# A PSUM bank for every other matmul: two output chunks of a weight tile computed in turn

## Chip, cores and metric

The kernel runs on one core of a Trainium2 chip. The metric is the device time of one execution in microseconds (us); lower is better. TensorE is the matmul engine (PE in the profile, its weight loads are PEld), DVE is VectorE, ACT is ScalarE, POOL is GpSimd, and SP issues the weight transfers.

## The reference

What is computed is a chain of layers on 512 tokens of width 1024, all in fp32, each added to x:

```python
x = x + gated_deltanet_mixer(rms_norm(x, a_norm), ...)      # A: 8 heads, w_in then w_out
k_band, v_band = shared_kv(x, kv_norm, w_kv, k_gain)        # KV
x = x + swa_sink_mixer(rms_norm(x, b_norm), ...)            # B: 32 heads, w_in then w_out
x = x + 0.5 * swiglu_ffn(rmsnorm(x, g), w_in, w_out)        # FF 0
x = x + pool_mixer(rmsnorm(x, g), ...)                      # pool
x = x + 0.5 * swiglu_ffn(...)                               # FF 1
x = x + 0.5 * swiglu_ffn(...)                               # FF 2
x = x + conformer_conv(rmsnorm(x, g), ...)                  # conv: pw1 (I), depthwise, pw2 (O)
x = x + 0.5 * swiglu_ffn(...)                               # FF 3
return rmsnorm(x, final_g)

def swiglu_ffn(x, w_in, w_out):
    gate, up = jnp.split(x @ w_in, 2, axis=-1)
    return (jax.nn.silu(gate) * up) @ w_out
```

## The kernel before

Activations lie transposed in SBUF, channels on partitions and the 512 tokens along the free dimension: x is xT, eight chunks of 128 channels. Weights stream through as tiles of 128 x 2048 (1 MB) in two buffers. Every tile goes through the same steps: SP loads it (`load`, L325 to L328), ACT rounds it to fp32r in w_hi (`round_tile`, L335), DVE forms the rest w_lo (`split_tile`, L340), and TensorE multiplies. A product of two fp32 numbers is made of three fp32r matmuls: hi by hi, hi by lo and lo by hi (L359, L360, L361 in `products`).

There are two kinds of tile, and TILES lists their order. An input tile (I) holds 256 output channels of x @ w_in over the whole depth of 1024: two output chunks, each of eight terms, so 2 x 24 matmuls. Its chunks go to PSUM banks 0 and 1, those of the next input tile to 2 and 3. An output tile (O) holds 256 rows of w_out and all 1024 output channels: eight chunks, each of two terms, so 8 x 6 matmuls, into banks 4 to 7 in turn. A feed-forward layer (FF) is I I, then ten times I I O, then O; the two I of a step are the gate and the up tile.

`pe_tile` (L364) issues both kinds, one chunk after the other. Each finished chunk raises chunk_done. Its readers wait for chunk_done: for an output chunk DVE adds it to xT (`add_chunks`, L402, or L400 with a bias) and raises out_free; for FF input chunks ACT takes silu of the gate (L1583) and DVE multiplies (L1625), which raises in_free. TensorE waits for out_free before a chunk n of an output tile, so that the chunk four before it, in the same bank, has been added, and for in_free before an input tile, with all_free for all banks. Two other places compute input tiles: `arriving` (L346 to L351) for the first tile of a layer, which takes each term as its h arrives and does three matmuls for one bank and three for the other; and `pe_filler` (L680 to L682), which places single terms between other work in A and B. Neither is touched.

After the last output tile of a layer the next norm begins: ACT squares each chunk of xT (L433), DVE sums the squares (`dve_sum`, L465, one after every add from the third chunk on, and L472 for the last), TensorE sums over partitions (`pe_stat`, L440), ACT takes the root (L457), DVE inverts and widens (L478, L480), TensorE spreads (L447), and DVE and ACT make h (L499, L510, L503).

All engines run their own program in order. In A's output tiles DVE has convolution taps (L1017, L1020) between adds 4 to 7 of the first tile and a weight split before the adds of the second; in FF and PW2 (the four output tiles of the convolution module) a split stands between adds 1 and 2.

Of the kernel before, what the change touches and what calls it, by code (L numbers as in the profile page):

```python
# [14 lines left out]
P = 128  # L15
D = 1024
# [51 lines left out]
CHUNK_CREDIT, SPLIT_CREDIT, IN_CREDIT, OUT_CREDIT = 1, 2, 4, 8  # L68
# [6 lines left out]
def in_before(t):  # L75
    return 2 * TILES[:t].count("I")
# [6 lines left out]
def pairs_before(t):  # L83
    return TILES[:t].count("O")


def at(f, t, i, period):

    return f(t) if i is None else i * (f(t + period) - f(t)) + f(t)
# [64 lines left out]
def build(nc, x, a_norm, a_w_in, a_conv, a_A_log, a_dt_bias, a_o_gain, a_w_out, kv_norm, w_kv,  # L154
# [4 lines left out]
    with ctx:  # L159
        def sb(name, shape, dt=F32, into=ctx):  # L160
            return into.enter_context(nc.sbuf_tensor(name, shape, dt))

        def sem(name):
            return ctx.enter_context(nc.semaphore(name))
# [3 lines left out]
        h_hi = sb("h_hi", [P, KC, T], F32R)  # L168
        h_lo = sb("h_lo", [P, KC, T], F32R)
# [3 lines left out]
        a_hi = sb("a_hi", [P, 2, 2, T], F32R)  # L173
        a_lo = sb("a_lo", [P, 2, 2, T], F32R)
# [102 lines left out]
        ps = ctx.enter_context(nc.psum_tensor("ps", [P, 8, T], F32))  # L277
# [5 lines left out]
        chunk_done = sem("chunk_done")  # L283
        in_free = sem("in_free")
        out_free = sem("out_free")
# [69 lines left out]
        def products(dst, terms):  # L355

            for k, (wh, wl, xh, xl) in enumerate(terms):
                last = k == len(terms) - 1
                nc.tensor.matmul(dst, wh, xh, start=(k == 0), stop=False)  # L359
                nc.tensor.matmul(dst, wh, xl, start=False, stop=False)  # L360
                m = nc.tensor.matmul(dst, wl, xh, start=False, stop=last)  # L361
            return m

        def pe_tile(pe, t, i=None, period=0, h_from=None, all_free=False):  # L364
            kind, slot = TILES[t], t % 2
            pe.wait_ge(lo_done, at(lambda u: u + 1 + SPLIT_CREDIT, t, i, period))
            wh, wl = w_hi[:, slot], w_lo[:, slot]
            if kind == "I":
                bank = 2 * ((in_before(t) // 2) % 2)

                pe.wait_ge(in_free, at(in_before, t, i, period) + (IN_CREDIT if all_free else IN_CREDIT - 2))
                if h_from is not None:
                    arriving(pe, h_from, wh, wl, (bank, bank + 1))
                    return
                for c in range(2):
                    terms = []
                    for k in range(KC):
                        w = slice(k * 256 + c * P, k * 256 + c * P + P)
                        terms.append((wh[:, w], wl[:, w], h_hi[:, k], h_lo[:, k]))
                    products(ps[:, bank + c], terms).then_inc(chunk_done, 1)  # L380
            else:
                pe.wait_ge(pair_ready, at(lambda u: pairs_before(u) + 1, t, i, period))
                buf = pairs_before(t) % 2
                for n in range(8):

                    pe.wait_ge(out_free, at(out_before, t, i, period) + (n - 4 + OUT_CREDIT + 1))
                    terms = []
                    for k in range(2):
                        w = slice(k * D + n * P, k * D + n * P + P)
                        terms.append((wh[:, w], wl[:, w], a_hi[:, buf, k], a_lo[:, buf, k]))  # L390
                    products(ps[:, 4 + n % 4], terms).then_inc(chunk_done, 1)

        def add_chunks(dve, t, ns, i=None, period=0, scale=1.0, bias=None, stat=None):

# [315 lines left out]
        def pe_a(pe, i):  # L710
# [133 lines left out]
            for k in (6, 7):  # L844
                pe_tile(pe, *a_tile_at(k, i))
# [1600 lines left out]
```

## Time and profile before

| what | value |
|---|---|
| three runs | 3039.43, 3043.0, 3044.31 us; median 3043.0 |
| profiled execution, span from first to last instruction | 3037.4 us (no other time of this execution is recorded) |
| TensorE matmuls, busy | 2862.0 us (94%), 13805 instructions |
| weight loads, busy | 2392.3 us (79%) |
| DVE busy | 1662.3 us (55%) |
| ACT busy | 948.7 us (31%) |
| chain that ended last | PE 85%, DVE 9%, issue 4%, ACT 2% |

TensorE's spans overlap: a matmul of 512 columns shows as 0.39 us, while the next starts 0.23 us after it. The price of one is therefore read from starts, not from busy time. A stage is read from the timeline, where each row has its start, its length, and in brackets the idle time of the engine before it with what ended that.

### The profile page before, as it was taken

What the parts mean: (1) busy time and instruction counts of PE and PEld (TensorE: products, weight loads), DVE (VectorE), ACT (ScalarE), POOL (GpSimd) and SP (SyncE); (2) the same over time, 40 slices, a digit from 0 to 9 for tenths busy, and PEclk for the clock granted to TensorE, in tenths of its full rate; (3) what the DMA queues carried; (4) which work ended last, traced back from release to release, by engine and by line L of the source; (5) the groups of instructions that cost most, each with busy time, mean ns of one, the idle gap of its engine ahead of it and who ended that gap; (6) DMA issues with size and microseconds to landing.
All of it is one profiled execution on the core that took longest, in us unless ns stands there. A gap on an engine that the chain in (4) does not pass through costs nothing.

```text
span 3037.4 us, 36977 instructions
## 1 busy us (share of the span) xinstructions
PE 2862.0 (94%) x13805; PEld 2392.3 (79%) x13805; DVE 1662.3 (55%) x2459; ACT 948.7 (31%) x1356; POOL 104.9 (3%) x119
## 2 busy tenths in 40 slices
PE   6999999998899998999997999999999897899998
PEld 5887878886788886788877888878888775688886
DVE  6546464645556566544456444454444799744445
ACT  4333242413454544322223222232222310432222
POOL 1000000000000000200000000000000142000000
PEclk9999999988999998999998999999999998899998
DMA  3111121200222221222221222222222210122221
GB/s 116 43 43 57 42 70 42 70 28 18 80 70 76 69 76 42 74 96 94 98 83 55 97 97 96 98 78 97 90 102 95 79 53 17 56 98 97 97 97 55
DMA packets 166620, 223.09 MB, mean 73 GB/s; under 512 B 5209, under 2 KB 148067, under 8 KB 166515
## 3 DMA queue, kind: packets, MB, share of 16 engines
q1 hardware_dynamic: 163523, 217.23, 21.8%
q0 software_dynamic: 1184, 4.24, 0.4%
q8 instruction: 68, 1.11, 0.2%
q10 hardware_dynamic: 1808, 0.21, 0.0%
q14 instruction: 37, 0.30, 0.0%
HBM read 219.51 MB, written 2.15 MB: 73 GB/s over the span
## 4 chain that ended last, share of the span: by engine, by line
PE 85%; DVE 9%; issue 4%; ACT 2%; DVEq 0%; POOL 0%; ACTq 0%; POOLq 0%
PE ps L359 18%; PE ps L361 18%; PE ps L360 18%; PE ps L680 4%; PE ps L682 4%; PE ps L681 4%; DVE w_lo L340 2%; PE ps L786 2%; PE ps L1378 1%; PE ps L769 1%; DVE dw_y L1936 1%; PE ps L1349 1%; PE ps L349 1%; PE ps L1367 1%; PE ps L350 1%
## 5 line engine op out<-in xcount | busy, mean ns | idle before, releaser
L335 ACT ACTIVATE w_hi<-w_raw 128x2048 fp32r<-128x2048 f32 x203 | 388.4, 1913 | 1084.3 <-PE ps L361 1071.0
L340 DVE TENSOR_TENSOR w_lo<-w_raw,w_hi 128x2048 fp32r<-128x2048 f32 x203 | 472.0, 2325 | 432.4 <-ACT w_hi L335 432.4
L359 PE MATMUL ps<-h_hi,w_hi 128*128 128x512 f32 x1472 | 573.7, 390 | 9.2 <-DVE glu L1905 3.6
L361 PE MATMUL ps<-h_hi,w_lo 128*128 128x512 f32 x1472 | 572.7, 389 | 0.0
L360 PE MATMUL ps<-h_lo,w_hi 128*128 128x512 f32 x1472 | 572.7, 389 | 0.0
L402 DVE SCALAR_TENSOR_TENSOR xT<-ps,xT 128x512 f32<-128x512 f32 x504 | 336.8, 688 | 169.1 <-PE ps L361 167.3
L359 PE MATMUL ps<-a_hi,w_hi 128*128 128x512 f32 x1024 | 403.3, 394 | 23.3 <-issue 13.2
L360 PE MATMUL ps<-a_lo,w_hi 128*128 128x512 f32 x1024 | 401.9, 392 | 0.0
L361 PE MATMUL ps<-a_hi,w_lo 128*128 128x512 f32 x1024 | 401.9, 392 | 0.0
L359 PEld LDWEIGHTS ps<-h_hi,w_hi 128*128 128x128 f32 x1472 | 276.3, 188 | 69.6 <-DVE f_hid L1625 5.0
L361 PEld LDWEIGHTS ps<-h_hi,w_lo 128*128 128x128 f32 x1472 | 276.3, 188 | 57.9
L360 PEld LDWEIGHTS ps<-h_lo,w_hi 128*128 128x128 f32 x1472 | 276.3, 188 | 57.2
L680 PE MATMUL ps<-h_hi,w_hi 128*128 128x512 f32 x608 | 259.8, 427 | 9.9 <-issue 4.5
L359 PEld LDWEIGHTS ps<-a_hi,w_hi 128*128 128x128 f32 x1024 | 194.5, 190 | 68.3 <-issue 21.5
L682 PE MATMUL ps<-h_hi,w_lo 128*128 128x512 f32 x608 | 241.8, 398 | 0.0
L681 PE MATMUL ps<-h_lo,w_hi 128*128 128x512 f32 x608 | 240.2, 395 | 0.0
L361 PEld LDWEIGHTS ps<-a_hi,w_lo 128*128 128x128 f32 x1024 | 194.2, 190 | 41.0
L360 PEld LDWEIGHTS ps<-a_lo,w_hi 128*128 128x128 f32 x1024 | 194.4, 190 | 40.3
L1625 DVE TENSOR_TENSOR f_hid<-f_gate,ps 128x512 f32<-128x512 f32 x88 | 60.5, 688 | 269.8 <-PE ps L361 269.8
L680 PEld LDWEIGHTS ps<-h_hi,w_hi 128*128 128x128 f32 x608 | 116.3, 191 | 38.1 <-issue 18.0
L682 PEld LDWEIGHTS ps<-h_hi,w_lo 128*128 128x128 f32 x608 | 115.8, 190 | 26.3
L681 PEld LDWEIGHTS ps<-h_lo,w_hi 128*128 128x128 f32 x608 | 116.8, 192 | 19.7
(307 smaller groups left out, 3154.8 us busy)
## 6 DMA issues: line engine op xcount, KB each, us to landing
w_raw<-in_ffn_w_in_dram SPq DMA_DIRECT2D x88, 1024.0 KB, 5.0
w_raw<-in_ffn_w_out_dram SPq DMA_DIRECT2D x44, 1024.0 KB, 4.9
w_raw<-in_a_w_in_dram SPq DMA_DIRECT2D x24, 1024.0 KB, 5.4
w_raw<-in_b_w_in_dram SPq DMA_DIRECT2D x16, 1024.0 KB, 5.4
w_raw<-in_conv_w_pw_dram SPq DMA_DIRECT2D x12, 1024.0 KB, 5.4
w_raw<-in_a_w_out_dram SPq DMA_DIRECT2D x8, 1024.0 KB, 4.9
w_raw<-in_b_w_out_dram SPq DMA_DIRECT2D x8, 1024.0 KB, 5.0
bias_cur<-rel_scratch POOLq DMA_DIRECT2D x8, 512.0 KB, 3.9
```

The lines of the kernel that those rows point to most:

```text
L335: nc.scalar.activation(w_hi[:, t % 2], w_raw[:, t % 2], ACT.Copy).then_inc(hi_done, 1)
L340: nc.vector.tensor_tensor(w_lo[:, t % 2], w_raw[:, t % 2], w_hi[:, t % 2].bitcast(F32), ALU.subtract).then_inc(lo_done, 1)
L349: nc.tensor.matmul(dst, wh[:, w], h_hi[:, k], start=k == 0, stop=False)
L359: nc.tensor.matmul(dst, wh, xh, start=(k == 0), stop=False)
L360: nc.tensor.matmul(dst, wh, xl, start=False, stop=False)
L361: m = nc.tensor.matmul(dst, wl, xh, start=False, stop=last)
L402: ins = nc.vector.scalar_tensor_tensor(xT[:, n], src, scale, xT[:, n], ALU.mult, ALU.add)
L680: nc.tensor.matmul(dst, wh[:, w], h_hi[:, k], start=k == 0, stop=False)
L681: nc.tensor.matmul(dst, wh[:, w], h_lo[:, k], start=False, stop=False)
L682: ins = nc.tensor.matmul(dst, wl[:, w], h_hi[:, k], start=False, stop=k == KC - 1)
L786: ins = mm(halves(pb(6 + a, c), l, 1), v(prod, a, c), halves(v(inv_T, a, c), l, 1), start=True, stop=True)
L1625: nc.vector.tensor_tensor(f_hid[:, c], f_gate[:, c], ps[:, 2 + c], ALU.mult).then_inc(in_free, 2)
```

## The change

`products_two` takes two chunks of a tile and issues for every term the three matmuls for both: hi by hi into the first bank, hi by hi into the second, hi by lo into the first, and so on. Both chunks raise chunk_done at the last two matmuls. `pe_tile` calls it for the two chunks of an input tile, and for chunks 0 and 1, 2 and 3, 4 and 5, 6 and 7 of an output tile; before each such pair it waits for out_free of the second. The matmuls and their number are the same.

```diff
--- before.py
+++ after.py
@@ -361,6 +361,19 @@
                 m = nc.tensor.matmul(dst, wl, xh, start=False, stop=last)
             return m
 
+        def products_two(dsts, terms):
+
+            n = len(terms[0])
+            for k in range(n):
+                last = k == n - 1
+                for part in range(3):
+                    for c in range(2):
+                        wh, wl, xh, xl = terms[c][k]
+                        ins = nc.tensor.matmul(dsts[c], (wh, wh, wl)[part], (xh, xl, xh)[part],
+                                               start=k == 0 and part == 0, stop=last and part == 2)
+                        if last and part == 2:
+                            ins.then_inc(chunk_done, 1)
+
         def pe_tile(pe, t, i=None, period=0, h_from=None, all_free=False):
             kind, slot = TILES[t], t % 2
             pe.wait_ge(lo_done, at(lambda u: u + 1 + SPLIT_CREDIT, t, i, period))
@@ -372,23 +385,24 @@
                 if h_from is not None:
                     arriving(pe, h_from, wh, wl, (bank, bank + 1))
                     return
+                terms = [[], []]
                 for c in range(2):
-                    terms = []
                     for k in range(KC):
                         w = slice(k * 256 + c * P, k * 256 + c * P + P)
-                        terms.append((wh[:, w], wl[:, w], h_hi[:, k], h_lo[:, k]))
-                    products(ps[:, bank + c], terms).then_inc(chunk_done, 1)
+                        terms[c].append((wh[:, w], wl[:, w], h_hi[:, k], h_lo[:, k]))
+                products_two((ps[:, bank], ps[:, bank + 1]), terms)
             else:
                 pe.wait_ge(pair_ready, at(lambda u: pairs_before(u) + 1, t, i, period))
                 buf = pairs_before(t) % 2
-                for n in range(8):
-
-                    pe.wait_ge(out_free, at(out_before, t, i, period) + (n - 4 + OUT_CREDIT + 1))
-                    terms = []
-                    for k in range(2):
-                        w = slice(k * D + n * P, k * D + n * P + P)
-                        terms.append((wh[:, w], wl[:, w], a_hi[:, buf, k], a_lo[:, buf, k]))
-                    products(ps[:, 4 + n % 4], terms).then_inc(chunk_done, 1)
+                for n in range(0, 8, 2):
+
+                    pe.wait_ge(out_free, at(out_before, t, i, period) + (n + 1 - 4 + OUT_CREDIT + 1))
+                    terms = [[], []]
+                    for c in range(2):
+                        for k in range(2):
+                            w = slice(k * D + (n + c) * P, k * D + (n + c) * P + P)
+                            terms[c].append((wh[:, w], wl[:, w], a_hi[:, buf, k], a_lo[:, buf, k]))
+                    products_two((ps[:, 4 + n % 4], ps[:, 4 + (n + 1) % 4]), terms)
 
         def add_chunks(dve, t, ns, i=None, period=0, scale=1.0, bias=None, stat=None):
```

In an output tile, TensorE's rows before, from the wait of a chunk to the wait of the next (w_hi, w_lo and a_hi, a_lo are the weight tile and the activations in their two parts):

```order
L359 MATMUL ps<-a_hi,w_hi 128x512 [waits out_free]
L360 MATMUL ps<-a_lo,w_hi 128x512
L361 MATMUL ps<-a_hi,w_lo 128x512
L359 MATMUL ps<-a_hi,w_hi 128x512
L360 MATMUL ps<-a_lo,w_hi 128x512
L361 MATMUL ps<-a_hi,w_lo 128x512
L386 REGISTER_ALU
L359 MATMUL ps<-a_hi,w_hi 128x512 [waits out_free]
```

and after, from the wait of a pair to that of the next. L372 is the one matmul line of `products_two`; x2 is one for each bank.

```order
L372 MATMUL ps<-a_hi,w_hi 128x512 [waits out_free]
L372 MATMUL ps<-a_hi,w_hi 128x512
L372 MATMUL ps<-a_lo,w_hi 128x512 x2
L372 MATMUL ps<-a_hi,w_lo 128x512 x2
L372 MATMUL ps<-a_hi,w_hi 128x512 x2
L372 MATMUL ps<-a_lo,w_hi 128x512 x2
L372 MATMUL ps<-a_hi,w_lo 128x512 x2
L399 REGISTER_ALU
L372 MATMUL ps<-a_hi,w_hi 128x512 [waits out_free]
```

The six matmuls between two waits have become twelve, and the first chunk is complete at the last but one of them. At the start of an input tile, before:

```order
L366 REGISTER_ALU
L371 REGISTER_ALU [waits lo_done]
L359 MATMUL ps<-h_hi,w_hi 128x512 [waits in_free]
L360 MATMUL ps<-h_lo,w_hi 128x512
L361 MATMUL ps<-h_hi,w_lo 128x512
L359 MATMUL ps<-h_hi,w_hi 128x512
```

and after:

```order
L379 REGISTER_ALU
L372 MATMUL ps<-h_hi,w_hi 128x512 [waits in_free,lo_done]
L372 MATMUL ps<-h_hi,w_hi 128x512
L372 MATMUL ps<-h_lo,w_hi 128x512 x2
L372 MATMUL ps<-h_hi,w_lo 128x512 x2
L372 MATMUL ps<-h_hi,w_hi 128x512 x2
```

In this tile, too, neighbours now differ in bank, and its first chunk is complete at the 47th matmul instead of the 24th.

## Rows read from the trace of the kernel before

**Rows 1.** Page, part 2: granted TensorE clock in tenths of full speed, 40 slices
```profile
PEclk9999999988999998999998999999999998899998
```

**Rows 2.** Page, part 5: groups of TensorE; busy us, mean ns | idle before
```profile
L359 PE MATMUL ps<-h_hi,w_hi 128*128 128x512 f32 x1472 | 573.7, 390 | 9.2 <-DVE glu L1905 3.6
...
L359 PE MATMUL ps<-a_hi,w_hi 128*128 128x512 f32 x1024 | 403.3, 394 | 23.3 <-issue 13.2
```

**Rows 3.** Timeline, TensorE, arriving tile: start us, us, engine, line, operation
```profile
2022.28 0.39 PE L350 MATMUL ps<-h_lo,w_hi 128*128 128x512 f32 x1
2022.51 0.40 PE L351 MATMUL ps<-h_hi,w_lo 128*128 128x512 f32 x1
2022.74 0.39 PE L349 MATMUL ps<-h_hi,w_hi 128*128 128x512 f32 x1
2022.97 0.40 PE L350 MATMUL ps<-h_lo,w_hi 128*128 128x512 f32 x1
```

**Rows 4.** Timeline, TensorE, the same tile at the lower clock
```profile
2018.44 0.63 PE L351 MATMUL ps<-h_hi,w_lo 128*128 128x512 f32 x1
...
2019.29 0.63 PE L350 MATMUL ps<-h_lo,w_hi 128*128 128x512 f32 x1
```

**Rows 5.** Timeline, TensorE, output tile: first matmuls of two chunks
```profile
1999.80 0.39 PE L359 MATMUL ps<-a_hi,w_hi 128*128 128x512 f32 x1
...
2001.16 0.39 PE L359 MATMUL ps<-a_hi,w_hi 128*128 128x512 f32 x1
```

**Rows 6.** Timeline, end of FF layer 1: TensorE, then DVE
```profile
2007.74 0.39 PE L361 MATMUL ps<-a_hi,w_lo 128*128 128x512 f32 x1
2010.39 0.84 PE L440 MATMUL ps<-ones,n_sum 128*128 128x1 f32 x6 [2.27 <-DVE n_sum L472]
...
2008.16 0.69 DVE L402 SCALAR_TENSOR_TENSOR xT<-ps,xT 128x512 f32<-128x512 f32 x1
2008.77 0.68 DVE L465 TENSOR_TENSOR n_sum<-n_sum,n_sq 128x512 f32<-128x512 f32 x1
2009.56 0.69 DVE L472 TENSOR_TENSOR n_sum<-n_sum,n_sq 128x512 f32<-128x512 f32 x1
```

**Rows 7.** Waits of TensorE: us in total, times, longest us
```profile
PE ps L440 <- DVE n_sum L472: 28.8, 9, 7.1
```

**Rows 8.** Timeline, DVE, the two output tiles of A's second iteration
```profile
410.52 3.12 DVE L402 SCALAR_TENSOR_TENSOR xT<-ps,xT 128x512 f32<-128x512 f32 x5
...
418.20 0.68 DVE L402 SCALAR_TENSOR_TENSOR xT<-ps,xT 128x512 f32<-128x512 f32 x1
...
420.12 2.28 DVE L340 TENSOR_TENSOR w_lo<-w_raw,w_hi 128x2048 fp32r<-128x2048 f32 x1
422.32 3.12 DVE L402 SCALAR_TENSOR_TENSOR xT<-ps,xT 128x512 f32<-128x512 f32 x5
```

**Rows 9.** Timeline, TensorE, the same two tiles
```profile
411.26 0.50 PE L359 MATMUL ps<-a_hi,w_hi 128*128 128x512 f32 x1 [1.77 <-DVE xT L402]
...
423.06 0.50 PE L359 MATMUL ps<-a_hi,w_hi 128*128 128x512 f32 x1 [0.63 <-DVE xT L402]
...
428.41 0.39 PE L361 MATMUL ps<-a_hi,w_lo 128*128 128x512 f32 x1
```

**Rows 10.** Timeline, head of FF layer 0: TensorE and DVE
```profile
1251.16 0.50 PE L359 MATMUL ps<-h_hi,w_hi 128*128 128x512 f32 x1 [0.84 <-DVE f_hid L1625]
...
1250.41 0.69 DVE L1625 TENSOR_TENSOR f_hid<-f_gate,ps 128x512 f32<-128x512 f32 x1 [4.64 <-PE ps L361]
```

**Rows 11.** Timeline, an output tile of the FF loop: DVE and TensorE
```profile
1991.93 1.28 DVE L402 SCALAR_TENSOR_TENSOR xT<-ps,xT 128x512 f32<-128x512 f32 x2
...
1994.36 0.39 PE L359 MATMUL ps<-a_hi,w_hi 128*128 128x512 f32 x1
```

**Rows 12.** Timeline, second output tile of PW2: DVE and TensorE
```profile
2616.54 2.48 DVE L402 SCALAR_TENSOR_TENSOR xT<-ps,xT 128x512 f32<-128x512 f32 x4
...
2617.77 0.39 PE L359 MATMUL ps<-a_hi,w_hi 128*128 128x512 f32 x1
```

## The prediction

> **What bounds the kernel now.** I read the page first. TensorE is busy for 94% of the span, and its granted clock stands at 9 tenths or more in 33 of 40 slices [rows 1]: the kernel is bound by TensorE at full clock (2.4 GHz), with short drops where layers meet. Part 5 says what fills it [rows 2]: L359, L360 and L361 on h_hi/w_hi (1472 each) and a_hi/w_hi (1024 each). These are the matmuls that the change reorders, 3 x (1472 + 1024) = 7488 of 13805. Loops at L349 to L351 and L680 to L682 stay as they are.
>
> The timeline then gives the price of one. Six matmuls of an output tile, one chunk, start 1.36 us apart from chunk to chunk [rows 5], 0.2267 us each, so the changed matmuls are 7488 x 0.2267 = 1697 us, 56% of the span. They follow one another without a gap; a term of the prediction is therefore either a change of this pitch or a gap that TensorE gets.
>
> **The pitch.** Does it matter that neighbours write different banks? The kernel before already has such neighbours. In the arriving tile, L349, L350, L351 write one bank and the next L349 the other. Starts are 0.23 us apart inside a bank (L349 to L350) and 0.23 across (L351 to L349) [rows 3]. In an output tile one step in six crosses a bank; were the crossing cheaper by 10 ns, the rows could show it only as 1.35 for 1.36, so the arriving tile is the better row, with one crossing in three. I take 0 for the change of pitch. The bounds: the same matmuls at the lower clock (1.2 GHz) take 0.85 us for two [rows 4], 0.425 each; at twice the clock the columns alone would be 0.2125, so at most 0.014 us is there to be won, 7488 x 0.014 = 105 us, if a fully alternating stream did what a single crossing doesn't. On the other side a switch could cost; the rows show none, and I put 1 ns (7.5 us) as what they cannot exclude.
> By the Trainium skill (TensorE: Matmul & The Clock Gate, Back-to-back issue gap) a warm 512-column matmul takes 512/2.4 + 2.5 = 215.8 ns; the trace's 226.7 disagrees, and by the page's figure the sum would hold an estimated gain of up to 7488 x 10.9 ns = 82 us if the difference came from the shared bank.
>
> **What moves.** The same 48 matmuls in a tile end at the same time, but both chunks of a pair now end together: the first 0.23 us before the second, where it ended half a pair earlier. DVE and ACT work on chunks in order, so work for the second queues behind that for the first. An add (L402) takes 0.61 us from start to start: five in 3.12 us [rows 8]. The second chunk's work is then 0.61 - 0.23 = 0.38 us later than before. Also TensorE now asks for both banks (out_free of n+1) before the first. By place:
>
> *Ends of layers.* After the last output tile TensorE waits for n_sum: 28.8 us, 9 times [rows 7]; seven of these follow a pe_tile output tile (A, B, four FFs, PW2). The last chunk's final matmul starts at 2007.74, its add at 2008.16 (0.42 later), and L472 at 2009.56, 1.40 after that add; TensorE resumes at 2010.39 [rows 6]. After the change chunk 6 ends at 2007.51; DVE does add 6, the square sum (0.60) that stands between the adds, then add 7: 0.61 + 0.60 - 0.23 = 0.98 us later. All behind it is a serial chain. 7 x 0.98 = +6.9 us.
>
> *Output tiles of A, three iterations with conv taps between the adds.* Here TensorE already waits for DVE. Chunk 4 starts at 411.26 [rows 9], 0.06 after add 0 ended (410.52 + 0.68 [rows 8]). Now chunks 4 and 5 need add 1, 0.61 later: 411.87. Chunk 4 ends with its 11th matmul, 411.87 + 10 x 0.2267 = 414.14, so add 4 starts at 414.56 instead of 412.96 (the fifth of the x5 row). From there DVE has no idle time through taps, add 7 (418.20), the split (420.12) and the second tile's adds (422.32): all are 1.60 later. The second tile's chunks 2 and 3 need add 7, which ends at 420.49 (0.5 us of waiting); chunks 4 and 5 need its add 1, ending 422.32 + 1.60 + 0.61 + 0.69 = 425.22, so they start at 425.28 (chunk 4 was 423.06 [rows 9]), and the 24 matmuls left put the last at 425.28 + 23 x 0.2267 = 430.49, where 428.41 stands: +2.1. What follows starts from TensorE (column sums, then root, then spread), so nothing absorbs it. 3 x 2.1 = +6.3 us. The last pair has no taps between, and no wait.
>
> *Output tiles of PW2.* For the second and third, DVE splits a weight tile between adds 1 and 2. Adds 2 and 3 begin at 2616.54 in a row of four; chunk 6 started at 2617.77 [rows 12] and needed add 2 alone. Now chunks 6 and 7 need add 3, ending 2616.54 + 0.38 + 0.61 + 0.68 = 2618.21: about 0.5 us of waiting, twice, +1.0.
>
> *FF loops, 40 output tiles.* The same condition: adds 2 and 3 begin at 1991.93, and chunk 6 starts at 1994.36 [rows 11]. Add 3 ends at 1993.21, with the shift at 1993.6, 0.76 us before it is needed. Nothing. The later split also issues the next 1 MB load up to 0.4 us later; a tile of 10.9 us covers it. If that cover were gone, it would be 0.4 us a tile.
>
> *FF heads.* The second gate tile (all_free) waits for both products: 0.84 us at 1251.16, behind the product of 1250.41 [rows 10]. That product now queues behind chunk 0's: 0.38 each, 4 x 0.38 = +1.5.
>
> *The rest.* The first pair of the conv stage, with sigmoid and product in series, +0.4, and the second KV tile, with two copies on ACT, +0.3, by the same 0.38. Conv's loop runs on DVE's taps, and the copies of the B loop have matmuls of the next step beside them: nothing. Fewer waits are issued (4 instead of 8 in an output tile); TensorE showed no gap for them, so nothing.
>
> Sum: 6.9 + 6.3 + 1.0 + 1.5 + 0.7 = +16.4 us. The profiled span of 3037.4 would be 3053.8. The median of the runs shown is 5.6 us above that span, and I carry this over: 3043.0 + 16.4 = **3059.4 us**, +0.5%.
>
> **Rivals.**
> *The pitch falls.* An accumulation into the bank that the matmul before still drains into could hold each one up, and only a stream without two in a row would be free of it. It decides from 16.4/7488 = 2.2 ns: at 224.5 ns the times are equal, below it the kernel is faster; the full 14 ns would give 3059.4 - 105 = 2954. For it: the warm matmul has time above its columns. Against it: single crossings [rows 3] get nothing of it. 8%.
>
> *The FF loops run out of slack.* If DVE is later by over 1.1 us when adds 2 and 3 come (0.38 are worked out), each of the 40 tiles makes TensorE wait; at 0.5 us each that is +20, 3079. For it: one slip recurs 40 times. Against it: the slack worked out [rows 11]. 12%. The Trainium skill (Perfetto Trace Analysis, Matmuls) says that independent groups should rotate through banks so that evacuating one overlaps the next one's matmuls; two groups that end together give this up within the pair, and by the rule the wait would show wherever DVE is full. The trace agrees for the end of a layer and has room in the loops.
>
> *The delays are absorbed.* If A's next iteration has slack that I do not see (its DVE copies wait for nothing of TensorE), and DVE takes the square sums of the layer ends in better time (0.5 each), 3.5 + about 1 remain: 3047. 8%.
>
> That the change does not do what it says is ruled out by the order of instructions.
>
> **How the numbers follow.** The forecast's own case, 72%, spans about 3052 to 3067: A between half and all (-3), 1 ns of pitch (+7.5), and 2 us of offset between runs. Some 0.2% (6 us) is what a measurement of this kernel can tell from no change. Faster by more than that: the falling pitch, 0.08. Within: the absorbed case and a little of the forecast's lower edge, 0.09. Slower: 0.83. The range reaches to 3045, which takes in most of the absorbed case, and to 3072, which takes in half of the loops' case.
>
> **What would show it.** Starts of the new line's matmuls 0.2267 us apart in the FF loops (1.36 for six); the wait for n_sum up by about 1 us for each of seven; in A, TensorE's waits for xT up from 0.6 and 1.8 us, with a third one at chunk 2 of the second tile; no gap in the FF loops. A pitch under 0.2245, or A's tiles ending less than 1 us later, would prove me wrong.

## The result and the profile after

Five runs of the changed kernel took 3052.43 to 3054.99 us, median 3053.84. Set against five runs of the kernel before on the same chip (median 3043.0), the ratio is 1.0047, with a 95% interval of 1.0035 to 1.0059: slower by 10.8 us, with 16.4 forecast. The profiled execution took 3052.43 us; its span is 13.4 us longer than that before. The median rose by less than the span, since the runs of either kernel scatter by some us; the account by terms at the end is of the spans.

The page of the changed kernel has the same shape as [rows 1] and [rows 2]:

```profile
span 3050.8 us, 36769 instructions
...
PE 2868.9 (94%) x13805; PEld 2395.5 (79%) x13805; DVE 1643.0 (54%) x2459; ACT 947.6 (31%) x1356; POOL 103.7 (3%) x119
...
PEclk8899999988999998999998999999999997899999
...
L372 PE MATMUL ps<-h_hi,w_hi 128*128 128x512 f32 x1472 | 454.4, 390 | 9.6 <-DVE f_hid L1639 5.3
L372 PE MATMUL ps<-a_hi,w_hi 128*128 128x512 f32 x1024 | 321.3, 395 | 28.4 <-issue 13.2
```

The mean of one is 390 ns, as before (395 for 394 in the output tiles). The busy sum of a group fell, from 573.7 to 454.4 us, only because two neighbouring matmuls of one group now overlap and the overlap is counted once; a busy sum is no price here. What decides is how many matmuls a full stretch holds. One window of the loop of FF layer 1, where TensorE has no gap, first in the kernel before, then in the changed one (columns: length, then the busy time and count of each engine, granted clock, DMA share, GB/s):

```profile
1703.00:2007.00 304.00, 304.00 (x1343) 251.73 (x1342) 138.24 (x147) 75.54 (x70) 0.00 (x0) 1.00 0.28 93
```

```profile
1703.00:2007.00 304.00, 304.00 (x1343) 251.73 (x1342) 134.51 (x146) 72.99 (x66) 0.00 (x0) 1.00 0.29 97
```

Both hold 1343 matmuls in 304.00 us at a granted clock of 1.00: 226.4 ns each, with and without alternation. So the time did not come from the matmuls of the loops but from waits. TensorE's waits in the changed kernel (total us, times, longest):

```profile
PE ps L454 <- DVE n_sum L486: 34.5, 9, 6.8
...
PE ps L372 <- DVE xT L416: 9.0, 11, 1.7
...
PE ps L372 <- DVE f_hid L1639: 5.3, 4, 1.3
PE ps L1381 <- DVE probs L1539: 4.7, 4, 2.2
...
PE ps L372 <- DVE glu L1919: 4.0, 2, 2.1
...
PE ps L694 <- issue: 0.9, 2, 0.5
```

and those of the kernel before that answer to them, beside [rows 7]:

```profile
PE ps L680 <- issue: 4.5, 2, 2.6
...
PE ps L1367 <- DVE probs L1525: 4.0, 3, 2.2
...
PE ps L359 <- DVE xT L402: 4.0, 6, 1.8
PE ps L359 <- DVE glu L1905: 3.6, 2, 1.9
...
PE ps L359 <- DVE f_hid L1625: 3.4, 4, 0.8
```

At the places that the change bears on five waits grew and one shrank: n_sum +5.7, xT +5.0, f_hid +1.9, probs +0.7, glu +0.4, and the idle time named issue (TensorE waited for nothing that the profile shows) at L680, L694 in the changed kernel, -3.6. This last one I had not foreseen, and the second set of runs is about it. Other waits moved too, by less than 0.5 us up (row_max 1.4 to 1.8, h_lo 24.0 to 24.3) and by more down (w_lo 2.2 to 0.2, glu_lo 8.5 to 6.9, n_rb 12.6 to 11.9, dw_y 8.8 to 8.2); the account by terms comes back to why a wait's total is a poor price.

At the end of FF layer 1, where [rows 6] stood before, DVE (first six rows) and TensorE (the last) now show:

```profile
2011.14 0.68 DVE L479 TENSOR_TENSOR n_sum<-n_sum,n_sq 128x512 f32<-128x512 f32 x1
2012.05 0.69 DVE L416 SCALAR_TENSOR_TENSOR xT<-ps,xT 128x512 f32<-128x512 f32 x1 [0.23 <-PE ps L372]
2012.66 0.68 DVE L479 TENSOR_TENSOR n_sum<-n_sum,n_sq 128x512 f32<-128x512 f32 x1
2013.26 0.68 DVE L416 SCALAR_TENSOR_TENSOR xT<-ps,xT 128x512 f32<-128x512 f32 x1
2013.86 0.68 DVE L479 TENSOR_TENSOR n_sum<-n_sum,n_sq 128x512 f32<-128x512 f32 x1
2014.64 0.69 DVE L486 TENSOR_TENSOR n_sum<-n_sum,n_sq 128x512 f32<-128x512 f32 x1
...
2015.48 0.69 PE L454 MATMUL ps<-ones,n_sum 128*128 128x1 f32 x5 [3.25 <-DVE n_sum L486]
```

Add 6 at 2012.05, a square sum, add 7 at 2013.26, a square sum, the last sum: the serial chain that the prediction drew up. TensorE's wait went from 2.27 to 3.25 us.

Loop A, second iteration, is where [rows 8] and [rows 9] were read. TensorE's waits, and behind them DVE, in the changed kernel:

```profile
403.96 0.72 PE L372 MATMUL ps<-a_hi,w_hi 128*128 128x512 f32 x2 [2.04 <-DVE a_lo L1010]
412.05 0.73 PE L372 MATMUL ps<-a_hi,w_hi 128*128 128x512 f32 x2 [0.75 <-DVE xT L416]
420.85 0.73 PE L372 MATMUL ps<-a_hi,w_hi 128*128 128x512 f32 x2 [0.35 <-DVE xT L416]
425.58 0.73 PE L372 MATMUL ps<-a_hi,w_hi 128*128 128x512 f32 x2 [1.71 <-DVE xT L416]
431.81 0.49 PE L694 MATMUL ps<-h_hi,w_hi 128*128 128x512 f32 x1 [0.47 <-issue]
```

```profile
414.87 0.69 DVE L416 SCALAR_TENSOR_TENSOR xT<-ps,xT 128x512 f32<-128x512 f32 x1 [1.68 <-PE ps L372]
...
420.12 0.68 DVE L416 SCALAR_TENSOR_TENSOR xT<-ps,xT 128x512 f32<-128x512 f32 x1
...
422.04 2.28 DVE L340 TENSOR_TENSOR w_lo<-w_raw,w_hi 128x2048 fp32r<-128x2048 f32 x1
424.24 2.48 DVE L416 SCALAR_TENSOR_TENSOR xT<-ps,xT 128x512 f32<-128x512 f32 x4
```

and TensorE at the top of the next iteration in the kernel before:

```profile
430.72 0.49 PE L680 MATMUL ps<-h_hi,w_hi 128*128 128x512 f32 x1 [1.92 <-issue]
```

From the first matmul of the two output tiles to the end of the last it was 403.76 to 428.80 (430.72 less 1.92), 25.04 us; now it is 403.96 to 431.34, 27.38 us: +2.34. But the next iteration, behind the branch back to the loop's top (the loop-back), begins 26.96 us after the first matmul in the one and 27.85 in the other: +0.89 only. The loop-back gave 1.45 us back.

### The profile page after: what moved, and what is told of

Same layout as the page of the kernel before. It is cut to its first block, busy times and chain, and to the rows that moved or that the text cites. A ratio compares the mean times of both kernels' runs of the same rounds, so it can differ in the third digit from the quotient of the medians.

```text
span 3050.8 us, 36769 instructions
## 1 busy us (share of the span) xinstructions
PE 2868.9 (94%) x13805; PEld 2395.5 (79%) x13805; DVE 1643.0 (54%) x2459; ACT 947.6 (31%) x1356; POOL 103.7 (3%) x119
## 4 chain that ended last, share of the span: by engine, by line
PE 84%; DVE 10%; issue 4%; ACT 2%; DVEq 0%; DMA 0%; SPq 0%; ACTq 0%
PE ps L372 53%; PE ps L694 4%; PE ps L696 4%; PE ps L695 4%; DVE w_lo L340 2%; PE ps L800 2%; PE ps L1392 1%; PE ps L783 1%; DVE dw_y L1950 1%; PE ps L349 1%; PE ps L1381 1%; PE ps L350 1%; PE ps L1363 1%; PE ps L351 1%; PE ps L808 1%
## 5 line engine op out<-in xcount | busy, mean ns | idle before, releaser
L372 PE MATMUL ps<-h_hi,w_hi 128*128 128x512 f32 x1472 | 454.4, 390 | 9.6 <-DVE f_hid L1639 5.3
L372 PE MATMUL ps<-h_hi,w_lo 128*128 128x512 f32 x1472 | 454.0, 390 | 0.0
L372 PE MATMUL ps<-h_lo,w_hi 128*128 128x512 f32 x1472 | 453.9, 389 | 0.0
L416 DVE SCALAR_TENSOR_TENSOR xT<-ps,xT 128x512 f32<-128x512 f32 x504 | 325.2, 684 | 197.9 <-PE ps L372 197.9
L372 PE MATMUL ps<-a_hi,w_hi 128*128 128x512 f32 x1024 | 321.3, 395 | 28.4 <-issue 13.2
L372 PEld LDWEIGHTS ps<-h_hi,w_hi 128*128 128x128 f32 x1472 | 276.1, 188 | 69.9 <-DVE f_hid L1639 7.0
L372 PEld LDWEIGHTS ps<-h_hi,w_lo 128*128 128x128 f32 x1472 | 276.7, 188 | 57.8
L372 PEld LDWEIGHTS ps<-h_lo,w_hi 128*128 128x128 f32 x1472 | 276.6, 188 | 57.6
L372 PE MATMUL ps<-a_hi,w_lo 128*128 128x512 f32 x1024 | 319.3, 393 | 0.0
L372 PE MATMUL ps<-a_lo,w_hi 128*128 128x512 f32 x1024 | 318.7, 393 | 0.0
L694 PE MATMUL ps<-h_hi,w_hi 128*128 128x512 f32 x608 | 259.9, 428 | 6.4 <-ACT conv_in L873 4.0
L372 PEld LDWEIGHTS ps<-a_hi,w_hi 128*128 128x128 f32 x1024 | 193.9, 191 | 75.3 <-issue 21.4
L696 PE MATMUL ps<-h_hi,w_lo 128*128 128x512 f32 x608 | 241.5, 397 | 0.0
L695 PE MATMUL ps<-h_lo,w_hi 128*128 128x512 f32 x608 | 240.4, 395 | 0.0
L372 PEld LDWEIGHTS ps<-a_lo,w_hi 128*128 128x128 f32 x1024 | 194.5, 190 | 41.1
L372 PEld LDWEIGHTS ps<-a_hi,w_lo 128*128 128x128 f32 x1024 | 194.3, 190 | 41.1
L694 PEld LDWEIGHTS ps<-h_hi,w_hi 128*128 128x128 f32 x608 | 116.2, 191 | 34.6 <-issue 14.4
```

Of the source, the lines that this page charges most:

```text
L372: ins = nc.tensor.matmul(dsts[c], (wh, wh, wl)[part], (xh, xl, xh)[part], start=k == 0 and part == 0, stop=last and part == 2)
L416: ins = nc.vector.scalar_tensor_tensor(xT[:, n], src, scale, xT[:, n], ALU.mult, ALU.add)
L694: nc.tensor.matmul(dst, wh[:, w], h_hi[:, k], start=k == 0, stop=False)
L695: nc.tensor.matmul(dst, wh[:, w], h_lo[:, k], start=False, stop=False)
L696: ins = nc.tensor.matmul(dst, wl[:, w], h_hi[:, k], start=False, stop=k == KC - 1)
```

## First set: is it the banks or the completion?

The changed kernel does two things at once: it alternates banks, and it completes the two chunks of a pair together. Four kernels take these apart.

**Input tiles only** alternate, in `pe_tile`:

```diff
-                for n in range(0, 8, 2):
-                    pe.wait_ge(out_free, at(out_before, t, i, period) + (n + 1 - 4 + OUT_CREDIT + 1))
...
-                    products_two((ps[:, 4 + n % 4], ps[:, 4 + (n + 1) % 4]), terms)
+                for n in range(8):
+                    pe.wait_ge(out_free, at(out_before, t, i, period) + (n - 4 + OUT_CREDIT + 1))
...
+                    products(ps[:, 4 + n % 4], terms).then_inc(chunk_done, 1)
```

> Only the input tiles (products of h_hi, h_lo; 4416 matmuls) alternate between two banks; the output tiles (3072 matmuls) are as before. Theory (only the completion of the pairs is later, alternation itself is free): the FF heads' gap goes from 0.84 to 1.32 us, four times (+1.9), the conv head +0.4, the second KV tile +0.3: +2.6 us, 3045.6, ratio 1.0009. The waits for n_sum stay at 28.8 us and loop A stays as before. Rival (the alternation itself costs, 10.8 us over 7488 matmuls or 1.4 ns each): 4416 x 1.4 ns = +6.4 us, ratio 1.0021, with no gap to show for it.

Measured: ratio 1.0011, interval 1.0002 to 1.002. Its waits:

```profile
PE ps L453 <- DVE n_sum L485: 28.7, 9, 7.1
...
PE ps L372 <- DVE f_hid L1638: 5.3, 4, 1.3
```

The time is the theory's; the rival's 1.0021 lies just outside the interval, so that the time alone would be thin evidence against it. The waits are firmer: f_hid has its 5.3 us, n_sum its old value, and the loop of FF layer 1 again holds 1343 matmuls in 304.00 us.

**Output tiles only** alternate:

```diff
-                terms = [[], []]
-                for c in range(2):
...
-                products_two((ps[:, bank], ps[:, bank + 1]), terms)
+                for c in range(2):
+                    terms = []
...
+                    products(ps[:, bank + c], terms).then_inc(chunk_done, 1)
```

> Only the output tiles (products of a_hi, a_lo; 3072 matmuls) alternate between two banks, and ask for two free banks at once; the input tiles are as before. Theory (late completion): the ends of the seven layers +6.8 us (waits for n_sum 34.5 us), loop A +3.4, PW2 +1.3, some of loop B's 1.0: +8 to +12 us, ratio 1.0027 to 1.004. The FF heads' gap stays at 0.84 us. Rival (the alternation costs 1.4 ns a matmul): 3072 x 1.4 ns = +4.4 us, ratio 1.0015.

Measured: 1.0029, interval 1.0018 to 1.004, at the lower end of the theory and above the rival. The two halves add up to 1.0040, within the interval of the whole. The wait for f_hid is back at 3.3 us, that for n_sum is 35.5.

**Last output tile serial**: the rest alternates.

```diff
+LAST_OUT = {T_KV - 1, T_FF[0] - 1, T_FF[3] - 1, *(f + 3 * FF_STEPS - 1 for f in T_FF)}
...
+                if t in LAST_OUT:
+                    for n in range(8):
+                        pe.wait_ge(out_free, at(out_before, t, i, period) + (n - 4 + OUT_CREDIT + 1))
...
+                        products(ps[:, 4 + n % 4], terms).then_inc(chunk_done, 1)
```

> As the changed kernel, but the last output tile of each of the seven layers is computed chunk after chunk, as before. Theory: the waits for n_sum return from 34.5 to 28.8 us or near it (3.25 to 2.27 us at each of the seven), and the kernel is 6.8 us faster than the changed one: about 4 us over the kernel before, ratio 1.0013. Rival (absorbed: what the wait gives back is lost to the low-clock stretch behind it, or the waits are not what the time is made of): 3053 us, ratio 1.0035 or more, while the waits are shorter.

Measured: 1.0028, interval 1.0016 to 1.0039; the median of 3047.61 is 6.4 us under that of the next kernel (3053.96), which ran on the same chip and has the changed kernel's time. The wait:

```profile
PE ps L465 <- DVE n_sum L497: 29.2, 9, 7.0
```

So the 6.8 us at the ends of layers are real time, and removable alone, as far as two medians with some 4 us of uncertainty between them can say. The ratio to the kernel before missed the 1.0013 that I had written, which lies below the interval; I had subtracted 6.8 from 10.8, where the waits of the changed kernel add up to more than 10.8.

**Late blocks**: no alternation, same completion.

```diff
-            for k in range(n):
-                last = k == n - 1
-                for part in range(3):
-                    for c in range(2):
-                        wh, wl, xh, xl = terms[c][k]
...
+            order = [(c, k, part) for c in range(2) for k in range(n) for part in range(3)
+                     if (k, part) != (n - 1, 2)] + [(0, n - 1, 2), (1, n - 1, 2)]
+            for c, k, part in order:
+                last = k == n - 1
+                wh, wl, xh, xl = terms[c][k]
```

> The changed kernel without its alternation: in each pair the first chunk's matmuls run in a block in one bank, then the second's in the other, and only the last matmul of each is held back to the pair's end. So both chunks complete, and both banks are asked for, exactly when they are in the changed kernel, and 7488 matmuls have two or three bank switches a pair in place of eleven or more. Theory (late completion): the same time as the changed kernel, 3053 to 3054 us, ratio 1.0035 to 1.0047; same waits for n_sum (34.5 us), same pitch of 226.7 ns. Rival (alternation costs): back to 3043 us, ratio 1.000. Second rival (alternation gains a little and hides part of the waits' cost): slower than the changed kernel, ratio over 1.006.

Measured: 1.0044, interval 1.0031 to 1.0057; median 3053.96 against 3053.84, span 3050.6 against 3050.8. Its waits for n_sum, xT, f_hid, probs and glu are those of the changed kernel to the last digit (the idle time at the loop-backs is 1.0 for 0.9):

```profile
PE ps L454 <- DVE n_sum L486: 34.5, 9, 6.8
...
PE ps L372 <- DVE xT L416: 9.0, 11, 1.7
PE ps L372 <- DVE f_hid L1639: 5.3, 4, 1.3
```

This settles the first question. In place of 11 bank switches in an output pair and 47 in an input pair it has three, and nothing else changed with them; its window 1703.00:2007.00 again holds 1343 matmuls in 304.00 us. One matmul more or less in that window would be 0.2 ns each, so **alternation as such neither costs nor gains anything that these traces show; all of the loss comes from the pair.** The pair does two things, which no kernel here separates in full: both chunks complete at its end, and TensorE asks for both banks at its start. By the rows, the ends of layers and the FF heads pay for the first, and the waits for xT in A and PW2 stand where the second asks for a later add.

## Second set: what did the loop-back give back?

TensorE's sequencer (PEldq in the profile) has records of its own, the branch among them, and runs ahead of the matmuls: when it takes the branch at 424.96, 3.83 us of them are left in the kernel before. My first idea was that it runs ahead only as far as its last held matmul, and that holding a pair instead of a single chunk let it start earlier on the branch. Two kernels tested this and, with it, a cure for A's waits.

**One wait moved**, on the kernel before, in A's second output tile alone:

```diff
-                    pe.wait_ge(out_free, at(out_before, t, i, period) + (n - 4 + OUT_CREDIT + 1))
+                    late = one_wait and n >= 6
+                    if not (late and n == 7):
+                        pe.wait_ge(out_free, at(out_before, t, i, period) + (n - 4 + OUT_CREDIT + 1 + late))
```

> The kernel before with one wait moved: in loop A's second output tile TensorE asks, ahead of chunk 6, for the bank of chunk 7 as well, and no longer ahead of chunk 7. Theory (at a loop-back TensorE's sequencer reaches the next iteration some 3.4 us after the last matmul that it had to hold behind a wait; in the changed kernel that is the first of twelve matmuls, 2.7 us of work, in the kernel before the first of six, 1.36 us): the idle time marked issue at the top of loop A shrinks by up to 1.36 us at each of two loop-backs, 1.9 to 0.5 us and 2.6 to 1.2 us: -2.7 us, ratio 0.9991. The price of asking early is nothing, since the add of chunk 3 ends 0.8 us before chunk 6 starts. Rival (the shorter idle time in the changed kernel came from its later end: the sequencer is simply ready at a fixed time after the loop's earlier work): no change, ratio 1.000, idle time of 1.9 us as before.

Measured: 1.0001, interval 0.999 to 1.0012; idle times of 2.57 and 2.79 us. The theory fell. The reason is in the trace: the branch starts 0.2 us after add 3 ends, whichever matmul waits for that add (chunk 7's in the kernel before: 424.80, branch at 424.96; chunk 6's here: 425.76 and 425.97). In the changed kernel it starts 0.47 us after it (426.72 and 427.19), so something else holds it there; what, was not tested.

**Early adds**, on the kernel before:

```diff
-            split(7)
             t, r, period = a_tile_at(6, i)
-            add_chunks(dve, t, range(0, 4), r, period)
+            early = 0 if last else 2
+            add_chunks(dve, t, range(0, early), r, period)
+            split(7)
+            add_chunks(dve, t, range(early, 4), r, period)
...
+            add_chunks(dve, t + 1, range(0, early), r, period)
             if not last:
                 split_tile(dve, 4 + NA, i, NA)
-            add_chunks(dve, t + 1, range(0, 8), r, period, stat=1 if last else None)
+            add_chunks(dve, t + 1, range(early, 8), r, period, stat=1 if last else None)
```

> The kernel before with VectorE's order changed in three iterations of loop A: the adds of chunks 0 and 1 of each of the two output tiles stand ahead of the split of the weight tile that they followed. Theory (TensorE waits there for banks 4 and 5 alone, 1.77 and 0.63 us): both waits go, -2.4 us an iteration, -7 us in three, ratio 0.9977; VectorE's idle time of 2.08 us ahead of the first split takes the adds. Rival (the split is late instead, and with it the weights of the next tile, or the loop-back's idle time grows by what the waits lose): -3 us or less, ratio 0.999 to 1.000.

Measured: 0.9989, interval 0.998 to 0.9998. The waits for xT went altogether, but the idle time at L680 grew from 4.5 to 7.9 us:

```profile
PE ps L680 <- issue: 7.9, 2, 4.0
```

The rival held: the loop-back took back most of what the waits gave. With **both edits**:

> The two edits together on the kernel before: early adds in loop A, and one wait for chunks 6 and 7 of its second output tile. Theory: the gains add, -7 and -2.7 us, ratio 0.9968. Rival (the loop-back is bound by something else than the last held matmul): as with the early adds alone.

Measured: 0.9992, interval 0.9983 to 1.0001: nothing added. And the **early adds on the changed kernel** (the same edit):

> The changed kernel with the same early adds in loop A. Theory (the waits of A's output tiles, 0.75, 0.35 and 1.71 us in an iteration, are for the adds of chunks 1 and 3 that stand behind a split): most of 2.8 us goes in each of three iterations, -7 to -8 us against the changed kernel, which leaves +3 us against the kernel before, ratio 1.0010, and the waits for n_sum stay at 34.5 us. Rival (the pairs' late completion alone makes these waits, whatever VectorE does first): -2 us or less, ratio 1.0035 or more.

Measured: 1.0046, interval 1.0032 to 1.006, so nothing gained. That is the rival's number, but not its reason: the waits for xT did fall, from 9.0 to 2.2 us, and the output tiles of A took 24.83 us in each of three iterations in place of 27.4. Instead the loop-backs' idle time rose to 3.30 and 3.03 us. That explains 5.4 of the 7.6 us; the rest is not accounted for. In all of these, something at the loop-back moved against me.

The record of the branch instruction names it. TensorE's sequencer, the branch at the end of loop A, in the kernel before, the changed one, and with early adds on each (durations in ns: least, median, most of three; the least is the one that falls through):

```profile
L2394 PEldq COMPARE_BRANCH  x3: 79/5497/6122, 256.3 to 591.5; - x3
```

```profile
L2408 PEldq COMPARE_BRANCH  x3: 79/4280/4360, 259.9 to 594.6; - x3
```

```profile
L2397 PEldq COMPARE_BRANCH  x3: 79/5877/6696, 257.0 to 592.3; - x3
```

```profile
L2411 PEldq COMPARE_BRANCH  x3: 79/5623/5936, 256.6 to 598.1; - x3
```

A taken branch of the FF loops takes 0.21 us, and one of loop B 0.22 to 0.24. In A it takes 4.3 to 6.7, while TensorE works off what is queued: at 424.96 the kernel before has 3.83 us of matmuls left and the branch takes 5.50, so TensorE idles for the rest and some 0.25 us of restart (1.92); the changed kernel has 4.14 left at 427.19 and takes 4.36 (0.47). What runs in that time, from the DMA queues in the window of a branch, second loop-back of the kernel before (424.96 to 430.46) and first of the changed one (259.90 to 264.18; packets, MB, share of 16 engines):

```profile
q1 hardware_dynamic: 825, 0.83, 44.0%
q8 instruction: 2, 0.03, 3.4%
```

```profile
q1 hardware_dynamic: 721, 0.72, 47.6%
q8 instruction: 1, 0.02, 1.6%
```

Queue 8 brings one or two packets of 16 KB of instructions, among some 700 to 800 packets of a weight tile on queue 1. In every trace so far the branch ends 1.3 to 1.9 us after the end of the last code packet; the long branches are those in which that packet came late. By the Trainium skill (Runtime: NRT & Kernel Launch, Instruction fetch mechanics) a taken branch whose target is not in the sequencer's current window has to fetch the page by DMA first. The trace agrees: A's body is the longest, with some 1070 of the sequencer's own records (weight loads, registers and the branch) an iteration against 610 in loop B and 318 in the FF loops, and only A's taken branches are long. Whether the fetch is slowed by the kernel's own transfers was tried next.

**Held load**, on the kernel before: the third weight tile of an iteration of A is loaded one split later, behind the loop-back.

```diff
-        def load(sp, t, src, i=None, period=0):
-            sp.wait_ge(lo_done, at(lambda u: u - 2 + SPLIT_CREDIT + 1, t, i, period))
+        def load(sp, t, src, i=None, period=0, hold=0):
+            sp.wait_ge(lo_done, at(lambda u: u - 2 + SPLIT_CREDIT + 1 + hold, t, i, period))
...
-                        load(sp, 6 + k, cols256(wi, bass.ds(i * 256 + c, 256)), i, NA)
+                        load(sp, 6 + k, cols256(wi, bass.ds(i * 256 + c, 256)), i, NA, hold=1 - k)
```

> The kernel before with one DMA held back: in each iteration of loop A the load of the third weight tile (1 MB) waits for one more split, that of the second tile, which stands behind the loop-back, so no weight load is under way when TensorE's sequencer takes the branch. In the kernel before that load is issued 2.4 us ahead of the branch, its packets are read until 2.3 to 4.4 us behind it, and the branch lasts 6.1 and 5.5 us with one or two 16 KB packets of queue 8 (kind: instruction) in it; in all traces so far it ends 1.4 to 1.8 us after the last of them. Theory (the loop-back's idle time is a load of code that is served among the packets of the weight load): the branch takes about 3 us, less than the 3.8 us of matmuls that are queued, and both idle times at the loop-backs (2.56 and 1.92 us) go: -4.2 us, ratio 0.9986. The load itself is needed 35 us later and costs nothing. Rival (the code load's time is its own, whatever else is read): branches of 5.5 us and ratio 1.000.

Measured: 0.9985, interval 0.9976 to 0.9993, as expected; the branches of 3.7 and 3.9 us are longer than the 3 that I had written. The branch, the one queue active in its second window, and all that is left of the idle time:

```profile
L2394 PEldq COMPARE_BRANCH  x3: 79/3722/3872, 256.0 to 587.3; - x3
```

```profile
q8 instruction: 1, 0.02, 2.2%
```

```profile
PE ps L680 <- issue: 0.4, 1, 0.4
```

**Early adds and held load** on the kernel before:

> Early adds and the held load together on the kernel before. With early adds alone both waits of A's output tiles went, but the idle time at the loop-backs grew to 4.0 and 3.8 us. Theory: these too come from the code load behind the weight load (issued 1.2 us ahead of the branch there) and go nearly to nothing: -6 to -7 us against the early adds alone, -9 to -11 us against the kernel before, ratio 0.9966. Rival (code load independent of the weight load): ratio 0.999 as with the early adds alone.

Measured: 0.9969, interval 0.9958 to 0.998; median 3029.1 us. The idle time is 2.8 us where it was 7.9 with the early adds alone:

```profile
PE ps L680 <- issue: 2.8, 2, 1.7
```

This kernel beats both of the case. I had written that the idle time would go nearly to nothing. What remains of it is the branch itself, 3.7 and 4.3 us, over a queue that is shorter now (2.92 us of matmuls) because TensorE isn't held up.

**Held load on the changed kernel**:

> The changed kernel with the same held load. Theory: its loop-backs cost only 0.42 and 0.47 us of idle time already (one packet of code in the branch, 4.3 us), so -0.9 us, ratio 1.0043; and the changed kernel is then 16 to 17 us slower than the kernel before with the held load, where it was 13.4 us slower span against span: the 3.6 us by which loop A came out cheaper than predicted were a gift of the loop-back. Rival (the 3.6 us were absorbed by something else): the difference to the kernel before with the held load stays at 13 us or less.

Measured: 1.0043, interval 1.003 to 1.0056. Its median of 3051.84 is 16.9 us above that of the kernel before with the held load (3034.95), on the same chip: with the loop-back's gift taken from both, the change costs about what was forecast. The ratios carry 3 and 4 us of uncertainty, so that the rival's 13 is not excluded by the medians. The traces speak against it: the branches take 3.6 to 3.9 us in both kernels, and in the second iteration it is 25.18 us from the first matmul of the output tiles to the next iteration in the one (399.81 to 424.99) and 27.20 in the other (401.58 to 428.78): +2.0, where it was +0.9 without the held load.

**Early adds and held load on the changed kernel**:

> The changed kernel with the early adds and the held load together. With early adds alone it did not get faster (three waits of 0.75, 0.35 and 1.7 us became one of 0.35, but the branches grew from 4.3 to 5.9 and 5.6 us, and the loop-backs' idle time from 0.45 to 3.3 and 3.0 us). Theory (that idle time is code behind the weight load, and A's waits were VectorE's order): both go, so 7 to 9 us against the changed kernel, 3045 us, ratio 1.0015 to 1.0022; and against the early adds and the held load on the kernel before (0.9969) what is left is the ends of layers 6.8, heads, conv and KV 2.6, PW2 1.3, loop B 1.0 and A 3 x 0.35 = 12.8 us. Rival (the pairs' late completion costs its 7.0 us in A whatever VectorE's order): 1.0043 as with the held load alone.

Measured: 1.0027, interval 1.0017 to 1.0036. The rival's 1.0043 is excluded. The early adds, worth nothing on the changed kernel while the load was in the way (1.0047 to 1.0046), seem worth 0.16% once it is not (1.0043 to 1.0027), some 5 us, though these two ratios come from different chips and their intervals overlap. I had written 1.0015 to 1.0022, so the gain is the theory's in kind and a little less in size. The output tiles with their waits last 24.83, 23.19 and 24.80 us in the three iterations, at a mean granted clock of 0.93, 1.00 and 0.93, in place of 27.4.

All branches of loop A that were taken, in the fourteen kernels, by what the trace shows in them (ahead: us from the load's issue to the branch):

```
weight load             code packets   branch, us
none                    1              3.34 3.42 3.58 3.70 3.72 3.73 3.87
none                    2              4.33
issued 2.4 to 2.7 ahead 1              4.20 4.28 4.30 4.36 4.36 4.43 4.54 4.59 4.76
issued 2.4 to 2.7 ahead 2              5.50 6.11 6.12 6.34 6.45
issued 1.2 to 1.3 ahead 1              5.62 5.66 5.88 5.93 5.94
issued 1.2 ahead        2              6.70
```

With one packet, that packet starts 1.0 to 1.5 us behind the branch where no weight load is under way, 1.7 to 2.3 us with one issued 2.4 to 2.7 us ahead, and 3.1 to 3.4 us with one issued 1.2 to 1.3 us ahead. In these traces the code packet comes later the more of the weight load is still to be read.

## Why the prediction was right, and where it was not

**The pitch: 0 taken, 0 found.** 1343 matmuls in 304.00 us in both kernels, and the late blocks gave the same time with three switches a pair. The falling pitch (8%) is excluded; the estimate of 82 us that stood beside it, from the Trainium skill's 215.8 ns (TensorE: Matmul & The Clock Gate, Back-to-back issue gap), fell with it: the shared bank is not what separates that figure from the measured 226.4 ns. What does is open.

**Ends of layers: +6.9 forecast, 6.9 found.** Six of the seven waits went from 2.27 to 3.24 us, 0.975 each, and PW2's from 2.33 to 3.37. The wait row shows only +5.7 for all nine, since the two that follow no output tile of `pe_tile` came out 1.2 us shorter together, one of them the first wait of the kernel. With the last output tiles serial again, 6.4 us came back.

**Loop A: +6.3 forecast, +3.4 found. This is the step that failed.** The output tiles themselves took 2.34 us more an iteration (forecast 2.1), with the third wait at the second tile's chunk 2 where it was drawn (0.35 for 0.5). The step that failed is the sentence that "nothing absorbs it". Behind the last matmul stands the loop-back, and its idle time of 2.56 and 1.92 us was there to be read in the profile of before; I took the column sums for what follows. The branches shrank from 6.12 and 5.50 us to 4.28 and 4.36, and gave back 3.6 us in two of three iterations. With 3.4 for A the sum would have been 13.5. One of the signs that I had named came out half: the waits for xT of 0.6 and 1.8 us became 1.71 and 0.75. The second fell although its matmul started later, because TensorE ran the 24 matmuls ahead of it at a mean granted clock of 0.79, where it had been 1.00.

**PW2: +1.0 forecast.** The waits are 0.32 us at two places, and at each the matmuls fall back by 0.48 us, which is the 0.5 that was drawn; from the first matmul of its output tiles to the last it was 2596.08 to 2642.02 and is 2604.96 to 2652.41, +1.5. The other 0.5 was not traced.

**FF heads: 0.38 each forecast, 0.48 found** (0.84 to 1.32 us, four times, +1.9 for 1.5): DVE's product for the second chunk does queue behind the first's, and the first begins 0.60 us after the start of its chunk's last matmul (1251.30 to 1251.90), where it was 0.48 (1249.93 to 1250.41). Where these 0.12 us come from was not tested. Conv head and KV: +0.4 and +0.3, as forecast.

**FF loops: 0, and 0.** The rival of the slack running out (12%) is excluded: all four windows of the FF loops are gapless. **Loop B: 0 forecast, +1.1 found**, 0.7 in the waits for probs and 0.4 in those for row_max; I had said that its copies have matmuls beside them, and at these places they have too few.

**From the terms to the median.** Ends 6.9, A 3.4, PW2 1.5, FF heads 1.9, conv and KV 0.7, B 1.1: 15.5 us for a span that is 13.4 us longer. The errors of both signs (A 2.9 too high, PW2, heads and B 2.0 too low) partly cancelled in the sum, which is luck. For the 2.1 us that are left the traces show one cause that is large enough, the clock. From n_sum to the gap of the FF head, 112 matmuls, FF layer 0 took 34.45 us at a mean granted clock of 0.80 in the kernel before and 32.29 us at 0.84 in the changed one, 2.2 us back; FF layer 1 took 30.86 us at 0.83 and 31.96 at 0.80, 1.1 us lost. No term of the change stands in either. That these shifts add up to just the 2.1 us is not shown. The granted clock drops in short stretches whose place differs from trace to trace, and a drop ahead of a wait can cost nothing. The first half of A's first output tile in two iterations of the kernel before:

```profile
235.09:242.58 7.49, 7.32 (x25) 5.60 (x25) 5.32 (x7) 5.04 (x7) 0.00 (x0) 0.77 0.00 0
403.76:411.26 7.50, 5.73 (x24) 4.43 (x25) 5.32 (x7) 5.05 (x7) 0.00 (x0) 1.00 0.00 0
```

At a mean clock of 0.77 TensorE is busy for 7.32 us and waits for 0.17, at 1.00 it is busy for 5.73 and waits for 1.77; DVE frees the bank at 7.5 us either way. A wait's total, such as xT's +5.0 for 7.0 us of longer tiles, is therefore a poor price, and the distance between two fixed instructions a good one. The changed kernel's median stands 3.0 us above its profiled span, where I had carried over the 5.6 of the kernel before. That the medians lie 10.8 us apart and the profiled spans 13.4 is within what two such kernels scatter: runs of the kernel before ranged over 3032 to 3047 us in the sets above.

**The rival of absorbed delays (8%)** was half right: it had A at 3.5 us, near the 3.4 found, by "slack that I do not see", and there was such slack, in the loop-back; but the ends of layers gave nothing.

## What to carry to other kernels

Interleaving two accumulation groups makes both end at the end of the pair. If their reader works on them in order, a place where TensorE waits for that reader pays about one reader's step less one matmul (here 0.38 worked out and 0.48 us measured at the FF heads, or 0.98 us where a step stands between), and asking for both banks at once can cost more (2.3 us in a pair of A's output tiles); where it doesn't wait, nothing is paid, and nothing was to be gained from the banks. The idle time named issue behind the long loop's branch was a load of code here: look for one in such a place, try to keep big transfers away from it, and read it before claiming that a delay ahead of it is carried on.

## What the hardware showed unexpectedly

A taken branch back over a long loop body held TensorE's sequencer for 3.3 to 3.9 us with one 16 KB packet of code and no weight load under way, 4.2 to 4.8 with a 1 MB weight load issued 2.4 to 2.7 us ahead of it, and 5.6 to 5.9 with one issued 1.2 to 1.3 us ahead; with a second code packet it was 4.3 without a load and 5.5 to 6.7 with one. A taken branch in the shorter loops took 0.21 to 0.24 us. Holding back one load was worth 0.15%. Why the same program has sometimes one and sometimes two code packets in the branch (4.59 and 6.45 us in one run of the input-only kernel) stays open, and with it why the changed kernel's branch is shorter. It issues the load 0.3 us earlier ahead of the branch (2.7 for 2.4). All eight branches with the load 2.7 us ahead had one packet, and five of the six with 2.4 us had two; the sixth took 4.59 us, no longer than the eight, so the second packet looks like the larger part.
